# Hybrid decoder block: the last token tile's hidden values row by row, and half of the output sums left in PSUM

## The chip, the cores and the metric

The kernel runs on one core of a Trainium2 chip. The metric is the device time of one execution in microseconds, as the median over runs. The core has five engines with a queue each: TensorE (PE, matmuls; PEld is its weight load), VectorE (DVE), ScalarE (ACT), GpSimd (POOL) and SyncE (SP, which issues DMAs). Each engine works its instructions off in program order, and they wait for each other through semaphores.

## The reference

One decoder block on 1,024 tokens of width 1,024, in float32. The part that matters here is its last one, PEER, a retrieval of experts. Each token is normed to `x`. Eight heads each make a query of 256 numbers, score it against two sets of 128 keys, take the best 16 of each set, and of their 256 sums the best 16. A pair of keys names one of 16,384 experts, so a token has 8 x 16 = 128 picks, with softmax weights `g` in each head:

```python
h = jnp.einsum('td,ted->te', xc, jnp.take(u, ic, axis=0))   # one row of u per pick
a = jax.nn.gelu(h, approximate=False) * gc
return jnp.einsum('te,ted->td', a, jnp.take(v, ic, axis=0)) # one row of v per pick
```

## The kernel before

The 1,024 tokens are eight tiles of 128. Tiles 0 and 1 (`NS = 2`) are done pick by pick: for each of the 128 picks, an indirect DMA fetches a row of `u` for each token (128 rows of 4 KB, 512 KB), and VectorE multiplies by `x` and sums, a "row job"; the same again with rows of `v`. That is 2 x 2 x 128 = 512 row jobs. The other six tiles (768 tokens, `DSEQ`) are done densely: every one of the 128 expert tiles (128 rows of `u` and of `v`) is multiplied with all 768 tokens, in two halves of 384 columns (`DHALF`), and a dense table of weights, mostly zero, selects. A float32 product is three float16 matmuls (`split_mm`, lines 238 to 240). So an expert tile costs 2 x 8 x 3 = 48 matmuls of 384 columns for the hidden values and 36 of 512 columns for the output `y`.

The stages that the change touches run one after another:

- `retrieve` (about 650 to 1055 us of the span). For each head `h` TensorE makes the queries and scores of head `h + 1` while VectorE finds the best 16s of a head. Between them lie 24 expert tiles (`HEAD_TILES`, 2 or 3 for a head and 6 for the last), whose hidden values are computed early, passed through gelu and stored to DRAM. One early tile goes: 8 transposes (`turn`), ScalarE writes the high part and the whole (`split`), GpSimd subtracts for the low part (`low`, line 1423), two halves of 24 matmuls (`hidden`), two gelus. GpSimd's queue for a head is: `low` of the first tile, `low_w` (low part of a query weight, line 1671), `picks` of the head before (line 1678, two products of 2,048 elements), then `low` of each further tile, with `weights` of the head before (line 1683) behind the second. VectorE waits for `weights` of the head before at line 1783.
- `spread_weights` (about 1055 to 1588 us). The dense table is built for four tokens at a step, 192 steps. VectorE makes `same`, `right` and two `left` tiles (lines 1892 to 1898), TensorE multiplies them (line 1918), ScalarE copies them out (line 1965). VectorE may be four steps ahead of TensorE (`RING`). With every four steps goes one early expert tile, 48 in all, handled as above.
- `experts` (from 1588 us). First 56 "late" tiles, whose hidden values are computed here, then the 72 early ones, whose hidden values are read back. Per tile VectorE also multiplies by the table (line 2366), makes low parts (lines 2315 and 2374), adds three finished `y` sums into `h` (`add_y`, line 2323), and does row jobs (lines 2332 and 2342): 2 for each early tile and the rest, 368, over the late ones. GpSimd makes `v_lo` (line 2301) and issues the row fetches (line 2292) into five buffers.

The `y` sums of a group of four tiles have two PSUM banks that take turns; each of the 12 sums of a group is added to `h` before its bank is used again.

## Time and profile before

| | |
|---|---|
| Median of 3 runs | 3084.58 us (3083.65 to 3088.66) |
| Profiled execution | 3081.31 us |
| Its span, first to last instruction | 3079.6 us |
| Mean granted TensorE clock | 0.983 of full |
| TensorE busy | 2968.7 us (96%) |
| VectorE busy | 2313.1 us (75%) |
| GpSimd busy | 1257.6 us (41%) |
| ScalarE busy | 977.5 us (32%) |

The profiled execution has 1.7 us outside its span, and lies 3.3 us under the median. Busy shares are means over stages with different limits, so the prediction reads each stage by itself. A matmul's length in the profile is longer than the distance to the next one, because matmuls overlap.

### The profile page before, as it was taken

The page shows a single profiled execution, that of the slowest core. Times are in us where ns is not written, and L with a number is a line of the kernel's source. Part 1 is how long each engine was busy: PE and PEld are TensorE (multiplying, and loading weights), DVE is VectorE, ACT ScalarE, POOL GpSimd, SP SyncE. Part 2 cuts the span into 40 slices and gives each one's busy share as a digit, 9 for nine tenths or more (in the row PEclk, how much of TensorE's full clock was granted, in tenths as well). Part 3 has the DMA queues.
Part 4 walks back from the last instruction along what each step waited for, and adds up shares of the span by engine and source line. Part 5 has one row for each costly group of instructions (what it writes and reads, how often), then busy time and mean ns, then how long its engine had stood idle before and what let it go on. Part 6 is the DMA issues. An engine that isn't in the chain of part 4 may idle for free. (4 is left out here: it accounts for less than half of the span.)

```text
span 3079.6 us, 46779 instructions
## 1 busy us (share of the span) xinstructions
PE 2968.7 (96%) x17450; PEld 1663.7 (54%) x17450; DVE 2313.1 (75%) x4663; ACT 977.5 (32%) x1417; POOL 1257.6 (41%) x883
## 2 busy tenths in 40 slices
PE   7989998989999799999999999999999999999999
PEld 4445465455555577777765555555555544444444
DVE  3255376358888666666649999989999999999996
ACT  4332365134433344444432222222222222222221
POOL 1013121014243311211226666676666666566562
PEclk9999899999999899999999999999999999999999
DMA  3110100121211245545568989989999888888884
GB/s 101 55 55 15 55 1 28 62 74 63 83 56 61 93 166 198 189 176 199 188 227 290 310 302 329 316 303 315 307 308 322 290 312 296 303 298 299 300 299 168
DMA packets 258490, 601.37 MB, mean 195 GB/s; under 512 B 21025, under 2 KB 127665, under 8 KB 255281
## 3 DMA queue, kind: packets, MB, share of 16 engines
q1 hardware_dynamic: 181168, 321.78, 31.0%
q0 software_dynamic: 73728, 268.47, 24.3%
q10 hardware_dynamic: 3456, 9.44, 0.8%
q8 instruction: 69, 1.13, 0.1%
q14 instruction: 69, 0.56, 0.1%
HBM read 516.78 MB, written 82.84 MB: 195 GB/s over the span
## 5 line engine op out<-in xcount | busy, mean ns | idle before, releaser
L238 PE MATMUL f_y<-f_v_hi,f_a_hi 128*128 128x512 f16 x1536 | 582.4, 379 | 8.7 <-DVE p_h L2323 8.7
L239 PE MATMUL f_y<-f_v_lo,f_a_hi 128*128 128x512 f16 x1536 | 582.1, 379 | 0.0
L240 PE MATMUL f_y<-f_v_hi,f_a_lo 128*128 128x512 f16 x1536 | 582.1, 379 | 0.0
L2292 POOL DMA_INDIRECT x_rows<-in_peer_v,p_row_index x256 | 305.9, 1195 | 281.6 <-DVE p_h L2342 256.2
L2292 POOL DMA_INDIRECT x_rows<-in_peer_u,p_row_index x251 | 321.7, 1282 | 186.4 <-DVE x_rows L2332 141.9
L2332 DVE SCALAR_TENSOR_TENSOR x_rows<-x_rows,p_xs 128x1024 f32<-128x1024 f32 x256 | 378.4, 1507 | 24.7 <-DMA x_rows<-in_peer_u,p_row_index 24.5
L2342 DVE SCALAR_TENSOR_TENSOR p_h<-x_rows,f_row_a,p_h 128x1024 f32<-128x1024 f32 x256 | 384.5, 1502 | 16.6 <-DMA x_rows<-in_peer_v,p_row_index 11.4
L2301 POOL TENSOR_TENSOR f_v_lo<-f_v_in,f_v_hi 128x1024 f16<-128x1024 f32 x128 | 286.8, 2241 | 87.4 <-ACT f_v_hi L2240 85.4
L2323 DVE SCALAR_TENSOR_TENSOR p_h<-f_y,p_h 128x512 f32<-128x512 f32 x384 | 262.4, 683 | 75.9 <-PE f_y L240 75.4
L238 PE MATMUL f_hid<-p_act_hi,x_u_hi 128*128 128x384 f16 x880 | 286.9, 326 | 2.1 <-DVEq L2308 2.1
L240 PE MATMUL f_hid<-p_act_hi,x_u_lo 128*128 128x384 f16 x880 | 286.9, 326 | 0.0
L239 PE MATMUL f_hid<-p_act_lo,x_u_hi 128*128 128x384 f16 x880 | 286.9, 326 | 0.0
L1894 DVE TENSOR_TENSOR e_right<-p_iota,p_picked_all 128x512 f16<-128x512 f32 x192 | 132.1, 688 | 188.0 <-PE e_tab L1918 188.0
L1423 POOL TENSOR_TENSOR e_u_lo<-e_u_all,e_u_hi 128x1024 f16<-128x1024 f32 x48 | 106.5, 2218 | 402.6 <-ACT e_u_all L1417 402.6
L238 PEld LDWEIGHTS f_y<-f_v_hi,f_a_hi 128*128 128x128 f16 x1536 | 150.2, 98 | 196.4 <-DVE p_h L2323 21.3
L238 PE MATMUL e_hid<-p_act_hi,e_u_hi 128*128 128x384 f16 x768 | 251.5, 327 | 4.1 <-POOL e_u_lo L1423 4.1
L239 PE MATMUL e_hid<-p_act_lo,e_u_hi 128*128 128x384 f16 x768 | 251.4, 327 | 0.0
L240 PE MATMUL e_hid<-p_act_hi,e_u_lo 128*128 128x384 f16 x768 | 251.4, 327 | 0.0
L240 PEld LDWEIGHTS f_y<-f_v_hi,f_a_lo 128*128 128x128 f16 x1536 | 150.3, 98 | 181.1
L239 PEld LDWEIGHTS f_y<-f_v_lo,f_a_hi 128*128 128x128 f16 x1536 | 150.3, 98 | 175.3
L2252 ACT ACTIVATE f_a_hi<-x_gel 128x768 f16<-128x768 f32 x128 | 107.6, 841 | 343.9 <-DVE x_gel L2366 343.9
L2240 ACT ACTIVATE f_v_hi<-f_v_in 128x1024 f16<-128x1024 f32 x128 | 134.9, 1054 | 214.8 <-DMA f_v_in<-in_peer_v 199.6
(314 smaller groups left out, 5489.5 us busy)
## 6 DMA issues: line engine op xcount, KB each, us to landing
f_v_in<-in_peer_v SPq DMA_DIRECT2D x128, 512.0 KB, 5.6
dense_weights<-e_stage SPq DMA_DIRECT2D x24, 2048.0 KB, 7.6
f_g_in<-dense_weights SPq DMA_DIRECT2D x32, 1536.0 KB, 16.2
x_u_in<-in_peer_u SPq DMA_DIRECT2D x56, 512.0 KB, 6.2
x_gel<-early_tiles SPq DMA_DIRECT2D x72, 384.0 KB, 3.5
e_u_in<-in_peer_u SPq DMA_DIRECT2D x48, 512.0 KB, 4.1
early_tiles<-e_gel SPq DMA_DIRECT2D x48, 384.0 KB, 2.3
a_w_in<-in_w_in SPq DMA_DIRECT2D x24, 512.0 KB, 3.7
```

Of the source, the lines that this page charges most:

```text
L238: pe.matmul(out, a_hi, b_hi, start=first, stop=False)
L239: pe.matmul(out, a_hi, b_lo, start=False, stop=False)
L240: return pe.matmul(out, a_lo, b_hi, start=False, stop=last)
L1423: self.nc.gpsimd.tensor_tensor(self.u_lo[b][:], self.u_all[:], self.u_hi[b][:], ALU.subtract).then_inc(self.u_lo_done, 1)
L1894: nc.vector.tensor_tensor(right[r][:], lanes(T.iota[:], 1, P, BANK_T, P), lanes(key1_t[:, toks], 2, P, BANK_T, P), ALU.is_equal)
L2240: nc.scalar.activation(v_hi[m // GROUP][m % GROUP][:], v_in[m % 2][:], ACT.Copy).then_inc(v_hi_done, 1)
L2252: nc.scalar.activation(a_hi[m // GROUP][m % GROUP][:], gel[m % 2][:], ACT.Copy).then_inc(a_hi_done, 1)
L2292: nc.gpsimd.indirect_dma_start(out=rows[q % ROWS][:], out_offset=None, in_=table, in_offset=bass.IndirectOffsetOnAxis(ap=T.row_index[:, ti ...
L2301: nc.gpsimd.tensor_tensor(v_lo[g][j][:], v_in[m % 2][:], v_hi[g][j][:], ALU.subtract).then_inc(v_lo_done, 1)
L2323: nc.vector.scalar_tensor_tensor(T.h[:, NS + t, cols], y[k % 2][:], 1.0 / S_A, T.h[:, NS + t, cols], ALU.mult, ALU.add).then_inc(y_added, 1)
L2332: nc.vector.scalar_tensor_tensor(row, row, 1.0, T.xs[:, tile, :], ALU.mult, ALU.mult, accum_out=row_hid[:, tile, pick:pick + 1]).then_inc( ...
L2342: nc.vector.scalar_tensor_tensor(T.h[:, tile, :], row, row_a[:, tile, pick:pick + 1], T.h[:, tile, :], ALU.mult, ALU.add).then_inc(row_use ...
```

## The change

1. The last token tile (tile 7, `HT`) leaves the dense product with `u`. The hidden matmuls of all 128 expert tiles go over 640 tokens (`HID`), in halves of 320 columns (`HHALF`). The output matmuls stay at six tiles.
2. Its 128 hidden values per token come from rows of `u`. The first 58 picks (`HELD_JOBS`) are done in `retrieve`, in heads 2 to 7, in up to five slots of two picks per head: GpSimd issues the fetch into one of two buffers and multiplies by `x` (`fetch`, `product`), ScalarE sums the row (`add_up`). The other 70 are row jobs of VectorE in the first 146 of the 192 steps of `spread_weights`. At the end of block 9 the values are passed through gelu, weighted, transposed and put in the place of tile 7's weights, so that the table holds finished values for these tokens; in `experts` ScalarE copies them (`held`).
3. In `spread_weights` the low part of an early tile is made by VectorE from PSUM, GpSimd only issues fetches, and the two `left` products are one instruction of twice the size.
4. In the early tiles of `experts`, the six `y` sums with odd `k` stay in PSUM banks freed by the hidden values (`resident`), over all groups, and are added to `h` once at the end. VectorE does 5 row jobs for two early tiles in place of 4, so 332 in place of 368 remain for the late tiles.

```diff
 # class EarlyTiles
-        toks = slice(NS * P + half * DHALF, NS * P + (half + 1) * DHALF)
+        toks = slice(NS * P + half * HHALF, NS * P + (half + 1) * HHALF)
...
+    def split_high(self, act, c, b):
+        n = c * self.ring + b
+        act.wait_ge(self.u_turned, n + 1)
+        act.wait_ge(self.hid_done, BASE + 2 * (n - self.ring) + 2)
+        self.nc.scalar.activation(self.u_hi[b][:], self.u_ps[:], ACT.Copy, scale=S_U).then_inc(self.u_hi_done, 1)
+
+    def low_from_bank(self, dve, c, b):
+        n = c * self.ring + b
+        dve.wait_ge(self.u_hi_done, n + 1)
+        self.nc.vector.scalar_tensor_tensor(self.u_lo[b][:], self.u_ps[:], S_U, self.u_hi[b][:], ALU.mult,
+                                            ALU.subtract).then_inc(self.u_lo_done, 1)
 # retrieve
+        def jobs(h, slot):
+
+            pair = (h - 2) * 5 + slot
+            return [q for q in (2 * pair, 2 * pair + 1) if 0 <= q < HELD_JOBS]
 # retrieve, ScalarE
+            def add_up(h, slot):
+                for q in jobs(h, slot):
+                    act.wait_ge(held_product, q + 1)
+                    nc.scalar.activation(rows[q % 2][:], rows[q % 2][:], ACT.Copy,
+                                         accum_out=T.h_hid[:, q:q + 1]).then_inc(held_sum, 1)
...
                 E.split(act, *of_head[0])
+                add_up(h - 1, 4)
                 if h + 2 < PEER_H:
                     split_w(h + 2, h % 2)
                 if h + 1 < PEER_H:
                     act.wait_ge(scored, 4 * h + 4)
                     queries_out(h + 1)
+                    add_up(h, 0)
                     scores_out(h + 1)
+                else:
+                    add_up(h, 0)
+                add_up(h, 1)
                 for i, (c, b) in enumerate(of_head):
...
                     E.keep(act, c, b)
+                    if i < 2:
+                        add_up(h, 2 + i)
 # retrieve, GpSimd
+            def fetch(h, slot):
+                for q in jobs(h, slot):
+                    pool.wait_ge(held_index, q // TOPK + 1)
+                    if q >= 2:
+                        pool.wait_ge(held_sum, q - 1)
+                    nc.gpsimd.indirect_dma_start(
+                        out=rows[q % 2][:], out_offset=None, in_=io.peer_u[0],
...
+            def product(h, slot):
+                for q in jobs(h, slot):
+                    pool.wait_ge(held_loaded[q % 2], 16 * (q // 2 + 1))
+                    nc.gpsimd.tensor_tensor(rows[q % 2][:], rows[q % 2][:], T.xs_h[:],
+                                            ALU.mult).then_inc(held_product, 1)
...
+                fetch(h, 0)
                 E.low(pool, *of_head[0])
+                product(h, 0)
+                fetch(h, 1)
                 if h + 2 < PEER_H:
                     low_w(h + 2, h % 2)
+                product(h, 1)
+                fetch(h, 2)
                 if h:
                     picks(h - 1)
                 for i, (c, b) in enumerate(of_head[1:]):
                     E.low(pool, c, b)
-                    if h and i == 0:
-                        weights(h - 1)
+                    if i == 0:
+                        product(h, 2)
+                        if h:
+                            weights(h - 1)
+                        fetch(h, 3)
+                    if i == min(1, len(of_head) - 2):
+                        product(h, 3)
+                        fetch(h, 4)
+                product(h, 4)
 # spread_weights, VectorE
-                nc.vector.tensor_tensor(left[r][:, 0], same[s % 2][:], each(w_hi), ALU.mult)
-                nc.vector.tensor_tensor(left[r][:, 1], same[s % 2][:], each(w_lo), ALU.mult).then_inc(built, 1)
...
+                nc.vector.tensor_tensor(left[r][:], lanes(same[s % 2][:], 1, P, 2, P, BANK_T),
+                                        lanes(w[:, :, toks], 2, P, 2, P, BANK_T), ALU.mult).then_inc(built, 1)
+
+                if n % 4 == 0 and n // 4 < EARLY_S * NBLOCK:
+                    E.low_from_bank(dve, *ring_at(n // 4 // EARLY_S, n // 4 % EARLY_S))
+                if n < JOB_STEPS:
+                    for q in range(UJOBS * n // JOB_STEPS, UJOBS * (n + 1) // JOB_STEPS):
+                        row_job(q)
 # spread_weights, TensorE
+            def turn_held(blk):
+                pe.wait_ge(h_a_done, 1)
+                pe.wait_ge(E.u_lo_done, BASE + (blk + 1) * EARLY_S)
+                pe.transpose(E.u_ps[:, 0, :], T.h_hid[:], T.ident[:]).then_inc(h_turned, 1)
+                pe.wait_ge(h_out, 1)
 # experts
+        resident = [u_ps[:].rearrange("p k c -> p (k c)")[:, h * HALF:(h + 1) * HALF] for h in range(2)] + [
+            hid_banks[b][:, h, :] for b in range(2) for h in range(2)]
...
-        LATE_JOBS = JOBS - SPREAD_JOBS - 2 * N_EARLY
+        LATE_JOBS = JOBS - SPREAD_JOBS - 5 * N_EARLY // 2
...
+                act.wait_ge(a_lo_done, BASE + n - 1)
+                nc.scalar.activation(gel[m % 2][:, HID:].rearrange("p (b t) -> p b t", t=TB),
...
+                stay = group_n >= RESIDENT
+                if stay and k % 2 and group_n < LAST:
+                    return
```

## Rows read from the trace of the kernel before

**Rows 1.** Windows of four stages: us, busy us (x instructions) of each engine.
```profile
654.00:1055.00 401.00, 382.56 (x2242) 224.83 (x2241) 344.55 (x1848) 148.47 (x191) 141.54 (x54) 1.00 0.19 66
1063.00:1574.00 511.00, 505.68 (x4218) 355.30 (x4217) 314.88 (x763) 239.45 (x383) 112.19 (x53) 0.99 0.50 185
1620.00:2470.00 850.00, 847.53 (x4738) 468.90 (x4736) 777.86 (x930) 187.76 (x209) 566.68 (x414) 1.00 0.91 309
2470.00:3060.00 590.00, 583.78 (x2692) 261.80 (x2691) 547.60 (x520) 135.79 (x145) 339.21 (x218) 1.00 0.83 290
```

**Rows 2.** The page's groups by cost, the two TensorE products.
```profile
L238 PE MATMUL f_y<-f_v_hi,f_a_hi 128*128 128x512 f16 x1536 | 582.4, 379 | 8.7 <-DVE p_h L2323 8.7
...
L238 PE MATMUL f_hid<-p_act_hi,x_u_hi 128*128 128x384 f16 x880 | 286.9, 326 | 2.1 <-DVEq L2308 2.1
```

**Rows 3.** Waits of the retrieval stage, 654 to 1055 us.
```profile
DVE r_weight L1783 <- POOL r_picked L1683: 35.7, 6, 7.8
```

**Rows 4.** Timeline of ScalarE, 843 to 896 us: start, length, operation.
```profile
865.41 0.60 ACT L1617 ACTIVATE r_q_t<-r_bank 128x512 f32<-128x512 f32 x1 [4.58 <-PE r_bank L240]
...
873.75 1.02 ACT L1415 ACTIVATE r_u_hi<-r_u_ps 128x1024 f16<-128x1024 f32 x1 [0.32 <-PE r_u_ps L1407]
```

**Rows 5.** Timeline of GpSimd, 840 to 945 us and at 1040 us.
```profile
846.86 2.14 POOL L1423 TENSOR_TENSOR r_u_lo<-r_u_all,r_u_hi 128x1024 f16<-128x1024 f32 x1 [11.11 <-ACT r_u_all L1417]
850.54 4.07 POOL L1671 TENSOR_TENSOR r_w_lo<-x_gr,r_w_hi 128x2048 f16<-128x2048 f32 x1 [1.54 <-ACT r_w_hi L1611]
854.57 7.62 POOL L1678 TENSOR_TENSOR r_match<-r_match,r_top_f 128x2048 f16<-128x2048 f16 x2
875.84 2.12 POOL L1423 TENSOR_TENSOR r_u_lo<-r_u_all,r_u_hi 128x1024 f16<-128x1024 f32 x1 [13.65 <-ACT r_u_all L1417]
...
885.08 2.13 POOL L1423 TENSOR_TENSOR r_u_lo<-r_u_all,r_u_hi 128x1024 f16<-128x1024 f32 x1 [6.76 <-ACT r_u_all L1417]
898.32 2.14 POOL L1423 TENSOR_TENSOR r_u_lo<-r_u_all,r_u_hi 128x1024 f16<-128x1024 f32 x1 [11.11 <-ACT r_u_all L1417]
...
941.95 2.67 POOL L1423 TENSOR_TENSOR r_u_lo<-r_u_all,r_u_hi 128x1024 f16<-128x1024 f32 x1 [12.17 <-ACT r_u_all L1417]
...
1040.40 2.12 POOL L1423 TENSOR_TENSOR r_u_lo<-r_u_all,r_u_hi 128x1024 f16<-128x1024 f32 x1 [7.12 <-ACT r_u_all L1417]
```

**Rows 6.** Timeline of GpSimd at the end of the spread.
```profile
1563.14 0.94 POOL L1994 DMA_INDIRECT x_rows<-in_peer_u,p_row_index  x1 [0.30 <-issue]
```

**Rows 7.** DMA issues: queue, count, us from issue to landing.
```profile
x_rows<-in_peer_u,p_row_index POOLq DMA_INDIRECT x256, 6.0
```

**Rows 8.** A window of 2 us at the start of the spread.
```profile
1074.00:1076.00 2.00, 2.00 (x8) 0.91 (x6) 0.00 (x0) 0.00 (x0) 0.45 (x1) 0.50 0.00 0
```

**Rows 9.** Timeline of VectorE in the spread, 1300 to 1323 us.
```profile
1302.85 0.69 DVE L1894 TENSOR_TENSOR e_right<-p_iota,p_picked_all 128x512 f16<-128x512 f32 x1 [1.49 <-PE e_tab L1918]
1303.46 0.42 DVE L1897 TENSOR_TENSOR e_left<-e_same,e_w_hi 128x512 f16<-128x512 f16 x1
1303.80 0.42 DVE L1898 TENSOR_TENSOR e_left<-e_same,e_w_lo 128x512 f16<-128x512 f16 x1
...
1304.47 0.68 DVE L1894 TENSOR_TENSOR e_right<-p_iota,p_picked_all 128x512 f16<-128x512 f32 x1
...
1313.32 0.69 DVE L1894 TENSOR_TENSOR e_right<-p_iota,p_picked_all 128x512 f16<-128x512 f32 x1 [1.49 <-PE e_tab L1918]
```

**Rows 10.** The chain of work that ended last, late tiles.
```profile
1650.73 0.87 PE f_u_ps L2173 x8
...
1667.17 0.87 PE f_u_ps L2173 x8
```

**Rows 11.** Timeline of VectorE in the late tiles, 1697 to 1712 us.
```profile
1702.02 1.23 DVE L2315 SCALAR_TENSOR_TENSOR x_u_lo<-f_u_ps,x_u_hi 128x1024 f16<-128x1024 f32 x1
1703.16 3.21 DVE L2332 SCALAR_TENSOR_TENSOR x_rows<-x_rows,p_xs 128x1024 f32<-128x1024 f32 x1
1706.31 0.08 DVE L2332 DVE_READ_ACCUMULATOR x_rows<-x_rows,p_xs 128x1 f32 x1
```

More of the change, by code:

```diff
@@ L1492, in retrieve @@
         picked = [S.sb(f"picked{n}", [P, NT, PICKS]) for n in range(3)]
+        rows = [S.sb(f"rows{b}", [P, D]) for b in range(2)]
         bank = [S.ps(f"bank{r}", [P, 4, NKEYS]) for r in range(4)]
@@ L1516, in retrieve @@
         all_out = S.sem("all_out")
+        held_index = S.sem("held_index")
+        held_loaded = [S.sem(f"held_loaded{b}") for b in range(2)]
+        held_product = S.sem("held_product")
+        held_sum = S.sem("held_sum")
         block = ctx.enter_context(nc.Block())
@@ L1909, in _, with step @@
             pe.sem_inc(spread, BASE)
-            def step(blk, last):
+            def turn_held(blk):
[3 more added lines that the diff above has]
+                pe.wait_ge(h_out, 1)
+            def step(blk, last, held=False):
                 for s in range(STEPS):
@@ L1929, in _ @@
             E.turn(pe, 0, 0)
-            with pe.Fori(0, NBLOCK - 1) as blk:
+            with pe.Fori(0, HBLOCK) as blk:
                 step(blk, False)
-            step(NBLOCK - 1, True)
+            step(HBLOCK, False, held=True)
+            for blk in range(HBLOCK + 1, NBLOCK):
+                step(blk, blk == NBLOCK - 1)
             def turn(b):
@@ L1966, in step @@
                                          tab[r][:].rearrange("p t i -> p i t"), ACT.Copy).then_inc(out, 1)
+                    if held and s == 3:
+                        gelu_held()
                     if s in HALVES:
@@ L2068, in experts @@
         u_ps = S.ps("u_ps", [P, KT, P])
-        hid = [S.ps(f"hid{b}", [P, 2, HALF])[:, :, 0:DHALF] for b in range(2)]
+        hid_banks = [S.ps(f"hid{b}", [P, 2, HALF]) for b in range(2)]
+        hid = [banks[:, :, 0:HHALF] for banks in hid_banks]
         y = [S.ps(f"y{b}", [P, HALF]) for b in range(2)]
@@ L2186, in hidden, with outputs @@
                 last.then_inc(hid_done, 1)
-            def outputs(group_n, g, part):
+            def outputs(group_n, g, part, stay=False, start=True, stop=False):
                 if part == 0:
@@ L2208, in step @@
                 if y_too:
-                    outputs(2 * c + m // GROUP - 1, (m // GROUP + 1) % 2, m % GROUP)
+                    outputs(2 * c + m // GROUP - 1, (m // GROUP + 1) % 2, m % GROUP, stay=early, start=first or not early)
             hidden(1, 1, between=2)
@@ L2218, in _ @@
                 step(LATE - 1, m, u_too=m < LOOP - 1)
-            with pe.Fori(LATE, TURNS) as c:
+            for m in range(LOOP):
+                step(LATE, m, early=True, first=m < GROUP)
+            with pe.Fori(LATE + 1, TURNS) as c:
                 for m in range(LOOP):
@@ L2222, in _ @@
             for part in range(GROUP):
-                outputs(NE // GROUP - 1, 1, part)
+                outputs(LAST, 1, part, stay=True, start=False, stop=True)
         @block.scalar
```

194 lines of the change are left out of this document (139 added, 55 removed).

## The prediction

> **What bounds the kernel now.** I read the page first, then cut the run into its stages by windows, because the busy shares of the page average over them. The windows [rows 1] give four stretches. In the retrieval TensorE is busy 382.6 of 401 us, in the spread 505.7 of 511, in the late tiles 847.5 of 850, in the early tiles 583.8 of 590. So TensorE bounds all four. The second engine differs: VectorE has 344.6 of 401 us in the retrieval, 314.9 of 511 in the spread, 777.9 of 850 and 547.6 of 590 behind it; GpSimd is nowhere a bound, but the reader should see that 141.5 us of 401 in the retrieval is little only as long as nobody waits for its order. The waits of that stage already show VectorE standing 35.7 us for GpSimd's `weights` [rows 3]. DMA takes 0.91 and 0.83 of its engines in the two expert stretches, at 309 and 290 GB/s [rows 1].
>
> **What a narrower hidden product gives.** A matmul of 512 columns lasts 379 ns and one of 384 columns 326 ns [rows 2]: 53 ns for 128 columns, 26.5 ns for the 64 that fall away. 48 matmuls make 1.27 us per expert tile, 163 us for 128 tiles, if TensorE stays the bound. That is the gross gain; the rest of the sum is what each stage gives back.
>
> **Retrieval: 24 tiles, minus 30 us of TensorE, plus 58 picks.** GpSimd gets 58 fetches, 1.24 us each (0.94 long and 0.30 to the next [rows 6]), and 58 products. No row has a float32 product of two SBUF tiles there; the nearest, `low` with the same 1,024 elements, is 2.13 us [rows 5], so I take that (bounds: 2.1, and 4.07, the length of `low_w` [rows 5]). ScalarE gets 58 sums; a copy of 1,024 elements lasts 1.02 us there [rows 4], and reading the sum out comes on top, I take 1.25 (VectorE's row job, product and all, is 1.22 [rows 11]). The busy time fits (58 x 3.4 = 196 us on GpSimd); the order does not. Each pair of fetches waits for the sums of the pair before, and these stand at fixed places in ScalarE's queue. I follow the head whose first `low` starts at 846.86 [rows 5], with all else at its old time. ScalarE has the last query bank out at 866.0 (the one at 865.41, 0.60 long [rows 4]) and only then sums slot 0: 867.2. GpSimd fetches slot 1 until 869.7, does `low_w` (4.07) until 873.8, the first row has landed after 6.0 us [rows 7] at 873.2, the products end at 878.1, and the second sum at 879.4. ScalarE stands in front of the first gelu until then. GpSimd waits with the second fetch of slot 2, until 880.6, then does `picks` (7.6 us [rows 5]), which before ran directly behind `low_w`. So `low` of the second tile starts at 888.2, not 875.84: TensorE is out of work from about 876 on and waits 12 us. The third tile: products of slot 2 to 894.6, sums to 895.9, gelu (0.5) and split (two copies of 1.0 [rows 4]) to 898.4, not 885.08. Two narrower halves of 3.3 us, turn and split later the next head's first `low` could start at 910.1, not 898.32: plus 12 us. A head with two tiles (898.32 to 941.95, 43.6 us) misses the last stretch: TensorE ends at 897, so the head takes 53, plus 9.5, but slots 3 and 4 are then still open, which hands 2.5 us to the next head. Heads 2 to 6 have 2, 3, 3, 2 and 3 tiles: 9.5 + 14.5 + 12 + 9.5 + 12.5 = 58. The last head has no queries that hide slots 0 and 1. Each is a round of fetch, landing, products and sum of about 10 us, and slot 2 comes on top: about 22 us until the `low` that stood at 1040.40. Heads 0 and 1 have no picks and gain 5 x 1.27 = 6. Sum: plus 74 us. What is late next: VectorE gets `weights` later by the same 16 us, but it then has a period of 63 us for its 43 us of work (344.6 in eight heads), so it isn't the bound.
>
> TensorE now stands idle twice in a head. After the idle stretch between the two stages the granted clock is 0.50, which is 1.2 GHz, and eight matmuls take 2 us even while it is fully busy [rows 8]. Most of the second tile's first half would be slow, but ScalarE is still at the sums then. I put 4 us for all heads. The Trainium skill (TensorE: Matmul & The Clock Gate, HAM oscillation) says that an array that waits in every round of a loop starts cold every round; by it I would put some 2 us on the path for each of eleven stalls, 22 us and not 4. The rows show such a cold spell at the stage's start, and no repeated one.
>
> **Spread: 48 tiles.** A tile with its four steps takes TensorE 1313.32 - 1302.85 = 10.47 us [rows 9]; less 1.27 is 9.2. VectorE needs 1.62 us for a step (1302.85 to 1304.47 [rows 9]), of which the two `left` are 0.34 each. One instruction of double size saves only a start: 0.60 for 0.68, step 1.54, four steps 6.2. The low part from PSUM is 1.14 (1702.02 to 1703.16 [rows 11]), and 70 x 4 / 146 = 1.92 row jobs of 1.15 (1.22 long, overlapping its successor by 0.07 [rows 11]) are 2.2. Sum 9.5: VectorE takes over as the bound by a little, for 36.5 tiles. 36.5 x 9.5 + 11.5 x 9.2 = 453 us against 48 x 10.47 = 503: minus 50. At the start GpSimd's slow first `low` goes, minus 4; at block 9 transpose and copy of the held values stop TensorE for some 2. Minus 52. If the merged product lost its rate, the nearest row is `right` with 0.61 for 512 elements, 1.2 for 1,024 [rows 9]. The skill (VectorE: DVE Perf Modes, What auto-detection actually checks) gives two elements a cycle to 16-bit tensors of step 1, which the merged one still is.
>
> **Late tiles.** The period is 1667.17 - 1650.73 = 16.44 us [rows 10], TensorE alone; it becomes 15.17. VectorE: 332/52 = 6.4 row jobs in place of 7.1, and one of them stretched by GpSimd's product (3.21 for 1.22 [rows 11]): 7.3 + 2.0 for rows, 1.8 for three `add_y`, 1.1, 0.75 and 0.9 for the others, 13.9 of 15.17, as tight as now. DMA: 512 KB each of `u` and `v`, 384 of the table and 6.4 x 512 of rows, 4.79 MB in 15.17 us, 316 GB/s where 309 stand now. 55 x 1.27 = 70, less 6 for slips: minus 64. ScalarE's `held` copy is hidden; its engine is busy 188 of 850 us [rows 1].
>
> **Early tiles.** 2,692 matmuls are 75 portions of 36 in 590 us, 7.9 us each, 99% TensorE. The resident sums take nothing from TensorE. They free 1.5 x 0.6 us of VectorE, which the half row job more (0.6) nearly takes back. Traffic rises to 2.56 MB in 7.9 us, 324 GB/s for 290. I take 0, bounds minus 5 and plus 68 (below).
>
> **Sum.** 74 + 4 - 52 - 64 = minus 38. 3081.3 - 38 = 3043; the median lies 3.3 above the profiled execution: 3047.
>
> **Rivals.** (a) The slots are covered: sums come out as soon as products end, and `picks` finds GpSimd free. For it speaks that GpSimd is idle 260 of 401 us. Against it the fixed place of the sums behind the query banks. The retrieval then keeps its gain of 30 us, at most plus 10: 2943 to 2983. (b) GpSimd's work is stretched by VectorE, which shares its ports: fetches of 2.0 us and products of 3.1. On the path of a head lie four fetches and six products, 10 us more in each of six: 3107, slower. It decides the sign from 6 us per head on. The stretched pair at 1703.16 [rows 11] speaks for it, but the best-16 searches that fill VectorE there have no second SBUF tensor. The skill's rule (GPSIMD Engine Reference, Engine selection) would put such products on VectorE, twice as fast; 58 x 1.15 = 67 us there, where 56 are idle. (c) DMA becomes the bound of `experts`: 4.79 MB at 309 GB/s is 15.5 us, plus 18 over the late tiles, and 2.56 MB at 290 is 8.8, plus 68 over the early: 3133; half of it 3090. (d) The merged product runs at half its rate: step 2.1 for 1.54, a tile 11.7, plus 82: 3129. (e) Gains and losses cancel within what a measurement can tell (0.2%, 6 us): 3078 to 3091.
>
> **Chances.** Forecast 0.52 (3020 to 3077); (a) 0.13; (b) 0.10; (c) 0.12, a third of it still faster; (d) 0.05; (e) 0.08. Faster 0.52 + 0.13 + 0.04 + a little of (b) = 0.71, same 0.08, slower 0.21. The range 2990 to 3105 leaves out most of (a), (d) and the full (c).
>
> **What would show it.** In the retrieval: GpSimd's second `low` of a head 12 us later after its first, ScalarE waiting for GpSimd products, TensorE busy under 80%, granted clock below 1.00. In the spread: a tile period near 9.5 with VectorE over 90% busy and TensorE waiting for it. Late period 15.2. Early period unchanged at 7.9 with DMA share over 0.9. Wrong it would be if the period of a middle head stayed at 51 us, or the early portions grew past 8.2.

## The result

| | Median | Range | Against before |
|---|---|---|---|
| Kernel before, same chip | 3086.27 us | 3083.65 to 3088.87 | |
| Kernel after | 3100.18 us | 3093.86 to 3106.81 | 1.0045 [1.0027, 1.0062] |

The change makes the kernel slower by 0.45%. The forecast was 3047 us and faster; the sign is wrong, the time lies near the upper end of the range. The profiled execution after took 3093.86 us, with a span of 3092.2.

The places in the trace where one stage hands over to the next tell where the time went. The starts are those of the spread's first table matmul, of the first hidden matmul of `experts` and of the last late one.

| Stage | before | after | difference | predicted |
|---|---|---|---|---|
| up to the spread's first table matmul | 1062.9 | 1158.3 | +95.4 | +78 |
| spread, to the first late hidden matmul | 527.1 | 470.9 | -56.2 | -52 |
| late tiles, first to last hidden matmul | 876.9 | 820.2 | -56.7 | -64 |
| the rest of the span, early tiles | 612.7 | 642.8 | +30.1 | 0 |
| sum (span) | 3079.6 | 3092.2 | +12.6 | -38 |

Each column comes from one profiled execution, and executions of one kernel differ. The first `low` of the retrieval starts at 655.9 us before and at 649.2 after, though the change does not touch what runs ahead of it; over the fourteen profiles of this document it starts between 648.4 and 657.7 us. So 6.7 us of the first row are scatter in the new kernel's favour: from first `low` to first table matmul the stage went from 407.0 to 509.1 us, plus 102.1.

### The profile page after: what moved, and what is told of

Same layout as the page of the kernel before. It is cut to its first block and busy times, and to the rows that moved or that the text cites. A ratio compares the mean times of both kernels' runs of the same rounds, so it can differ in the third digit from the quotient of the medians.

```text
span 3092.2 us, 46939 instructions
## 1 busy us (share of the span) xinstructions
PE 2828.5 (91%) x17451; PEld 1673.5 (54%) x17451; DVE 2371.1 (77%) x4563; ACT 1012.8 (33%) x1615; POOL 1418.8 (46%) x1021
## 3 DMA queue, kind: packets, MB, share of 16 engines
q8 instruction: 77, 1.26, 0.2%
## 5 line engine op out<-in xcount | busy, mean ns | idle before, releaser
L246 PE MATMUL f_y<-f_v_hi,f_a_hi 128*128 128x512 f16 x1080 | 410.7, 380 | 40.8 <-DVE f_a_lo L2561 33.5
L247 PE MATMUL f_y<-f_v_lo,f_a_hi 128*128 128x512 f16 x1080 | 410.7, 380 | 0.0
L248 PE MATMUL f_y<-f_v_hi,f_a_lo 128*128 128x512 f16 x1080 | 410.7, 380 | 0.0
L246 PE MATMUL f_hid<-p_act_hi,x_u_hi 128*128 128x320 f16 x880 | 264.6, 301 | 2.0 <-DVEq L2489 2.0
L247 PE MATMUL f_hid<-p_act_lo,x_u_hi 128*128 128x320 f16 x880 | 264.6, 301 | 0.0
L248 PE MATMUL f_hid<-p_act_hi,x_u_lo 128*128 128x320 f16 x880 | 264.5, 301 | 0.0
L246 PE MATMUL r_hid<-p_act_hi,r_u_hi 128*128 128x320 f16 x384 | 123.5, 322 | 128.0 <-POOL r_u_lo L1433 128.0
L246 PE MATMUL e_hid<-p_act_hi,e_u_hi 128*128 128x320 f16 x768 | 230.2, 300 | 0.0
L247 PE MATMUL e_hid<-p_act_lo,e_u_hi 128*128 128x320 f16 x768 | 230.2, 300 | 0.0
L248 PE MATMUL e_hid<-p_act_hi,e_u_lo 128*128 128x320 f16 x768 | 230.1, 300 | 0.0
L1745 POOL TENSOR_TENSOR r_rows<-r_rows,p_xs_h 128x1024 f32<-128x1024 f32 x58 | 136.3, 2360 | 23.7 <-DMA r_rows<-in_peer_u,p_h_index 23.4
```

Of the source, the lines that this page charges most:

```text
L246: pe.matmul(out, a_hi, b_hi, start=first, stop=False)
L247: pe.matmul(out, a_hi, b_lo, start=False, stop=False)
L248: return pe.matmul(out, a_lo, b_hi, start=False, stop=last)
L1745: nc.gpsimd.tensor_tensor(rows[q % 2][:], rows[q % 2][:], T.xs_h[:], ALU.mult).then_inc(held_product, 1)
```

## The profile after

First the windows of the stages, with the columns of [rows 1].

```profile
core 0: us, PE busy (x) PEld busy (x) DVE busy (x) ACT busy (x) POOL busy (x), PEclk, DMA share, GB/s
640.00:1140.00 500.00, 371.36 (x2251) 232.85 (x2250) 346.19 (x1853) 206.00 (x306) 331.53 (x168) 0.87 0.34 110
1160.00:1510.00 350.00, 342.14 (x3198) 271.52 (x3199) 350.00 (x615) 147.84 (x254) 65.56 (x70) 0.99 0.85 305
1510.00:1616.00 106.00, 105.22 (x1010) 84.18 (x1008) 84.42 (x150) 45.21 (x82) 0.00 (x0) 1.00 0.53 195
1630.00:2450.00 820.00, 807.50 (x4907) 487.43 (x4906) 731.70 (x902) 203.47 (x276) 521.03 (x382) 0.99 0.89 307
2450.00:3070.00 620.00, 586.48 (x2691) 262.93 (x2690) 537.02 (x448) 152.91 (x219) 402.50 (x254) 0.99 0.84 299
```

In the retrieval TensorE stands idle for 129 of 500 us, where it had 18 of 401 idle, and its mean clock is 0.87 in place of 1.00. No other engine is full either: GpSimd has 332 of 500. That is the picture of a wait, not of a bound. In the spread VectorE is busy 350 of 350 us: it is the bound, as forecast. In the early tiles TensorE falls from 99% to 94.6%, and the DMA share hardly moves, 0.84 for 0.83 [rows 1]. These windows hold the end of the stage too, where the loads run out. Without it, before and then after:

```profile
2480.00:3020.00 540.00, 534.54 (x2465) 239.60 (x2464) 510.15 (x482) 128.79 (x138) 323.60 (x207) 1.00 0.86 301
2480.00:3020.00 540.00, 510.69 (x2341) 228.84 (x2340) 469.94 (x391) 135.21 (x193) 360.13 (x227) 0.99 0.86 306
```

The share is the same 0.86, and 5 GB/s more go with TensorE at 94.6% for 99.0%.

The waits of the retrieval (waiting instruction, whom it waits for: us in all, times, the longest):

```profile
ACT r_rows L1670 <- POOL r_rows L1745: 155.6, 44, 11.3
PE r_hid L246 <- POOL r_u_lo L1433: 128.0, 17, 19.6
DVE r_weight L1862 <- POOL r_picked L1729: 119.6, 7, 26.6
POOL r_rows L1737 <- ACT r_rows L1670: 43.6, 22, 13.9
```

The 129 idle us of TensorE are one row, 128.0 us for GpSimd's `low`. ScalarE waits 155.6 us for products, in front of its own gelu and split. One head with two tiles (head 5), with the same columns as [rows 5]; its first `low` is at 941.43, the next head's at 1003.23:

```profile
941.43 2.14 POOL L1433 TENSOR_TENSOR r_u_lo<-r_u_all,r_u_hi 128x1024 f16<-128x1024 f32 x1
943.53 4.66 POOL L1745 TENSOR_TENSOR r_rows<-r_rows,p_xs_h 128x1024 f32<-128x1024 f32 x2
952.87 0.98 POOL L1737 DMA_INDIRECT r_rows<-in_peer_u,p_h_index  x1 [4.69 <-ACT r_rows L1670]
954.16 0.94 POOL L1737 DMA_INDIRECT r_rows<-in_peer_u,p_h_index  x1 [0.30 <-issue]
955.12 4.08 POOL L1717 TENSOR_TENSOR r_w_lo<-x_gr,r_w_hi 128x2048 f16<-128x2048 f32 x1
959.15 4.65 POOL L1745 TENSOR_TENSOR r_rows<-r_rows,p_xs_h 128x1024 f32<-128x1024 f32 x2
...
966.70 7.62 POOL L1724 TENSOR_TENSOR r_match<-r_match,r_top_f 128x2048 f16<-128x2048 f16 x2
974.26 2.13 POOL L1433 TENSOR_TENSOR r_u_lo<-r_u_all,r_u_hi 128x1024 f16<-128x1024 f32 x1
976.34 4.65 POOL L1745 TENSOR_TENSOR r_rows<-r_rows,p_xs_h 128x1024 f32<-128x1024 f32 x2
...
986.01 4.71 POOL L1745 TENSOR_TENSOR r_rows<-r_rows,p_xs_h 128x1024 f32<-128x1024 f32 x2 [2.13 <-DMA r_rows<-in_peer_u,p_h_index]
990.87 0.98 POOL L1737 DMA_INDIRECT r_rows<-in_peer_u,p_h_index  x1 [0.15 <-DVE p_h_index L1825]
992.67 1.87 POOL L1737 DMA_INDIRECT r_rows<-in_peer_u,p_h_index  x1 [0.82 <-ACT r_rows L1670]
995.43 2.35 POOL L1745 TENSOR_TENSOR r_rows<-r_rows,p_xs_h 128x1024 f32<-128x1024 f32 x1 [0.89 <-DMA r_rows<-in_peer_u,p_h_index]
997.96 2.35 POOL L1745 TENSOR_TENSOR r_rows<-r_rows,p_xs_h 128x1024 f32<-128x1024 f32 x1 [0.18 <-DMA r_rows<-in_peer_u,p_h_index]
...
1003.23 2.13 POOL L1433 TENSOR_TENSOR r_u_lo<-r_u_all,r_u_hi 128x1024 f16<-128x1024 f32 x1
```

The same two `low` of this head before:

```profile
927.29 2.13 POOL L1423 TENSOR_TENSOR r_u_lo<-r_u_all,r_u_hi 128x1024 f16<-128x1024 f32 x1 [13.64 <-ACT r_u_all L1417]
941.95 2.67 POOL L1423 TENSOR_TENSOR r_u_lo<-r_u_all,r_u_hi 128x1024 f16<-128x1024 f32 x1 [12.17 <-ACT r_u_all L1417]
```

The reader is to see two things. GpSimd waits 4.69 us with the second pair of fetches until ScalarE has summed the first pair, which stands behind the query banks, and `picks` then stands in front of `low`. Even so the second `low` comes only 3.8 us later after the first than before, 32.8 us for 29.0. The larger part of this head's loss lies behind it: 29.0 us to the next head's first `low` in place of 14.7, because the products of slots 2, 3 and 4 and their fetches all stand ahead of that `low`. Before, GpSimd waited 12 us for its data there; now it is busy 50.1 of the head's 61.8 us. ScalarE's split for the second `low` had been done at 967.1. While TensorE waits for that `low` the clock falls. Windows of 4 us, the clock is the third value from the end:

```profile
966.00:970.00 4.00, 0.00 (x0) 0.00 (x0) 0.00 (x0) 1.46 (x3) 3.99 (x2) 0.50 0.80 201
974.00:978.00 4.00, 1.55 (x6) 0.89 (x7) 0.00 (x0) 0.00 (x0) 4.00 (x3) 0.50 0.00 0
982.00:986.00 4.00, 4.00 (x33) 3.15 (x32) 3.97 (x5) 0.94 (x4) 1.53 (x2) 1.00 0.61 177
```

The page's chain of work that ended last, which here reaches back to the start of `experts`, shows the early tiles. After:

```profile
PE 18%; DVE 11%; DMA 10%; issue 6%; SPq 1%; ACT 1%; POOL 1%; DVEq 0%; ACTq 0%
```

Six of the ten per cent of DMA are the loads of `v`. Before, the same line of the page had PE 36% and DMA 4%.

## The experiments

Twelve kernels ran, in three groups. In each, the kernel before ran on the same chip (medians 3087.85, 3085.20 and 3086.78 us). "Spread at" is the first table matmul, "spread", "late" and "early" are the three other lengths of the table above, in us of the profiled execution. That execution is not always near the median: it lies 14.7 us above it in `order38` and 9 us below it in `order38_s` and `fit28`. The late and early columns differ by some 10 us between kernels that are alike there (818 to 830 and 642 to 651), so differences of that size say nothing by themselves.

| Run | Median | Ratio | Spread at | spread | late | early |
|---|---|---|---|---|---|---|
| before | 3086.27 | 1 | 1062.9 | 527.1 | 876.9 | 612.7 |
| after | 3100.18 | 1.0045 [1.0027, 1.0062] | 1158.3 | 470.9 | 820.2 | 642.8 |
| resident_only | 3126.19 | 1.0125 [1.0106, 1.0143] | 1066.3 | 526.9 | 875.9 | 658.0 |
| tile7_only | 3110.25 | 1.0079 [1.0060, 1.0099] | 1162.1 | 472.6 | 865.3 | 612.3 |
| half_v | 3076.66 | 0.9953 [0.9933, 0.9974] | 1165.7 | 472.5 | 830.2 | 609.6 |
| held28 | 3077.14 | 0.9970 [0.9955, 0.9986] | 1105.1 | 508.2 | 818.5 | 642.0 |
| order58 | 3086.03 | 1.0002 [0.9986, 1.0018] | 1146.7 | 472.4 | 819.3 | 647.2 |
| order38 | 3066.73 | 0.9938 [0.9917, 0.9960] | 1103.2 | 496.0 | 829.6 | 650.9 |
| held8 | 3074.26 | 0.9963 [0.9945, 0.9981] | 1073.0 | 531.9 | 826.3 | 647.6 |
| after_2jobs | 3103.68 | 1.0078 [1.0049, 1.0106] | 1154.0 | 472.4 | 862.6 | 605.7 |
| order38_s | 3048.25 | 0.9880 [0.9856, 0.9905] | 1083.3 | 494.3 | 818.0 | 642.0 |
| fit28 | 3046.96 | 0.9874 [0.9852, 0.9897] | 1065.5 | 508.1 | 819.0 | 643.3 |
| fit28_s | 3052.28 | 0.9888 [0.9867, 0.9910] | 1071.3 | 508.0 | 822.2 | 645.9 |
| left_split | 3115.95 | 1.0098 [1.0060, 1.0135] | 1160.8 | 482.3 | 821.2 | 645.8 |

### The two halves of the change apart

`resident_only` is the kernel before with the resident sums and their five row jobs for two early tiles; `tile7_only` is the kernel after without them.

```diff
 # tile7_only, against after
-        LATE_JOBS = JOBS - SPREAD_JOBS - 5 * N_EARLY // 2
+        LATE_JOBS = JOBS - SPREAD_JOBS - 2 * N_EARLY
...
 # and outputs, add_y and the final wait of SP as in before
```

> The kernel before with one part of the change alone: the six odd y sums stay in PSUM through the early tiles, and VectorE does 5 row jobs for two early tiles (332 for the late ones). The hidden products stay at 768 tokens, and the retrieval and the spread stay as they were. Traffic theory (the expert tiles are held by DMA at about 300 GB/s, the rate at which the early tiles ran in the kernel before, 2.36 MB in 7.9 us, and in the changed one, 2.56 MB in 8.5 us): an early tile moves 2.62 MB, so it takes 8.7 us and not 7.9, plus 60 us over 72 tiles; the late tiles stay at TensorE's 16.44 us; total about 3145. Order theory (the early tiles are held by GpSimd, VectorE and the load queue waiting for each other, and the resident sums relieve it; what slowed them in the changed kernel is the picks' side): the early tiles stay at 7.9 us, total 3080 to 3090.

> The changed kernel without the resident sums: all 12 y sums go through two banks as before, and VectorE does 4 row jobs for two early tiles, 368 for the late ones. Traffic theory: an early tile moves 2.29 MB, TensorE holds it again at 7.9 us, minus 42 us against the changed kernel; a late tile moves 5.15 MB, which at 310 GB/s takes 16.6 us where TensorE needs 15.17, so the late tiles take what they took before the change, plus 50 to 65 us; total 3105 to 3120. Order theory (late tiles are held by TensorE alone, which lost 1.27 us a tile): the late tiles stay at about 15.2 us and the early ones go back to 7.9, total about 3060.

Alone, the resident sums cost 45 us in the early tiles and give nothing in the late ones, though these have 36 row jobs less. Without them the early tiles run as before, 612.3 us, but the late tiles fall back to 865.3: of the 70 us that the narrower products give there, 12 are left. So each half does little without the other: the row jobs that leave the late tiles let the narrower products take effect, and cost time among the early ones. In all, the resident half is worth 10 us to the kernel with tile 7 (3110 against 3100). Both runs fit the traffic theory; of the two totals it wanted, 3105 to 3120 came (3110), and for about 3145 it was 3126, since the early tiles lost 45 us and not 60.

### Is it the traffic?

In `half_v` the loads of `v` from the second turn on bring only the first 512 of 1,024 columns, so half of `y` is built from stale rows; everything else is as in after. In `after_2jobs` only the number of row jobs goes back to four for two early tiles.

```diff
 # half_v
-                    sp.dma_start(v_in[m % 2][:], v_v[view, m]).then_inc(v_loaded[m % 2], 16)
+                    cols = slice(0, D if first else HALF)
+                    sp.dma_start(v_in[m % 2][:, cols], v_v[view, m][:, cols]).then_inc(v_loaded[m % 2], 16)
```

> The changed kernel, but in experts the load of a tile's v rows brings only the first 512 of the 1,024 columns from the second group of eight tiles on (the other half of the buffer keeps old values; this part of y is left wrong). No instruction less on any engine, 0.26 MB less in each tile. Traffic theory: early tiles 2.29 MB, back to 7.9 us; late tiles to 15.2; experts from 1463 to about 1415 us, total about 3050. Order theory: no change beyond the shorter landing of v, total 3090 to 3100.

> The kernel after with four row jobs to two early tiles, as before, in place of five; the sums stay resident. The late tiles get the 37 jobs. Traffic theory (at the bytes per tile of the kernel before the early tiles run as they did): early to end 610 to 618 us in place of 643, but the late tiles then carry the bytes of the run with tile 7 alone and go from 820 to about 865: 3100 to 3118, no gain, because the bytes of the whole stage decide. Order theory (the resident sums themselves, their places in TensorE's and VectorE's order, cost the early tiles their 30 us): early to end stays near 640, and with the slower late tiles the kernel takes 3135 to 3145.

The windows of the early tiles, first `half_v`:

```profile
2468.00:3060.00 592.00, 586.99 (x2718) 265.17 (x2716) 545.66 (x450) 152.29 (x219) 409.10 (x254) 1.00 0.83 282
```

then `after_2jobs`, late and early:

```profile
1628.00:2490.00 862.00, 819.58 (x4901) 489.20 (x4899) 781.99 (x937) 203.78 (x277) 552.55 (x416) 0.98 0.91 313
2490.00:3060.00 570.00, 568.59 (x2632) 256.62 (x2630) 493.50 (x408) 152.51 (x219) 335.86 (x220) 1.00 0.83 290
```

With half of each `v` load gone and nothing else changed, the early tiles take 609.6 us for 642.8, and TensorE is back at 99%. The resident sums and all row fetches are still there, and VectorE's busy time is the same (546 us of 592, 537 of 620). So the 30 us are the price of transfers, not of the order of the sums. The waits show the path. The first two rows are of the early tiles after (2450 to 3070 us), the last two of `half_v` (2468 to 3060):

```profile
PE f_y L246 <- DVE f_a_lo L2561: 33.5, 15, 3.5
DVE x_gel L2553 <- DMA x_gel<-early_tiles: 43.3, 17, 4.1
PE f_y L246 <- DVE f_a_lo L2562: 4.9, 6, 1.3
DVE x_gel L2554 <- DMA x_gel<-early_tiles: 18.1, 15, 2.1
```

TensorE waits for VectorE's low parts, and VectorE for the hidden values that are read back. In the chain of work that ended last, within the early tiles, the loads of `v` make up 28.9% after, 14.3% in `half_v` and 12.4% before. In `after_2jobs` the early tiles take 605.7 us with the resident sums in place, 7 less than before, so the order theory, which wanted 640, falls. For the traffic it says less than `half_v`, because with 36 row jobs go their 512 KB each as well as their time on VectorE: there VectorE waits even longer for the read values, 47.1 us, but is busy 494 of 570 us, catches up, and TensorE loses 1.3 us to it. `half_v` as a whole took 3077 us; about 3050 was wanted, since the late tiles gave nothing. What is taken out of the early tiles is paid in the late ones: plus 42.4 us for 36 row jobs, 1.18 us each. There the cause is left open: that is VectorE's own time for a row job (1.21 us) as well as 512 KB at 444 GB/s, `half_v` did not make the late tiles of the kernel after faster (830.2 for 820.2, within the scatter), and no run here gives the crowded late tiles of `tile7_only` less traffic alone.

### Fewer picks in the retrieval

```diff
-HELD_JOBS = 58
+HELD_JOBS = 28      # held8: 8
```

> The changed kernel with 28 picks of tile 7 in the retrieval (heads 2, 3 and four slots of head 4) and 100 in the spread in place of 58 and 70. Slot theory (each head with slots loses its 12 to 20 us because sums and products stand ahead of the gelu and of picks in their queues): heads 5, 6 and 7 return to the period of TensorE, 41 to 47 us and some 50 for the last, so the retrieval ends some 55 us earlier, while the spread takes 30 row jobs more at 1.15 us, plus 35; total 20 us less, about 3080. Rival (the loss is one of TensorE's clock and of GpSimd's load as a whole, spread over all heads): the retrieval gives back only its share of the picks' GpSimd time, 30 x 3.6 / 2, and the spread takes 35: no gain, 3095 to 3105.

> The kernel after with 8 picks in the retrieval in place of 58, in the old order, and 50 more row jobs in the spread. By held28 a pick in heads 5 to 7 cost 53 / 30 = 1.8 us of the retrieval and 37.5 / 30 = 1.25 us in the spread. If the slots of heads 3 and 4 cost as much, the spread starts at 1105 - 36 = 1069 and lasts 508 + 25 = 533: 3066. If the first 28 picks cost what they add up to against the kernel before (42 us plus the 30 us of narrower products, 72 / 28 = 2.6 us each), it starts at 1053: 3050. If fetches from memory bound the spread (rather than VectorE), its share passes 0.95 and it takes over 545 us: above 3080.

`held28` moves 30 picks of heads 5 to 7 to the spread: the retrieval gets 53.2 us shorter and the spread 37.3 longer, 1.77 us for a pick in the one and 1.24 in the other. Counted from each run's own first `low`, the retrieval is 57.2 us shorter, 1.91 for a pick. A pick in GpSimd's free time costs more of the kernel than one on the engine that bounds the next stage. The slot theory wanted about 3080, and 3077 came. `held8` does not go on like this: its spread starts at 1073.0 us and lasts 531.9, as its first branch had it (1069 and 533), and the kernel gains only 3 us more (3066 was wanted), within the two intervals. Its eight picks all stand in head 2, which has two tiles and still takes 63.8 us from first `low` to first `low` where it had 43.6: 2.5 us for a pick, more than the 1.8 of heads 5 to 7. With its fifth slot, in the kernel after, the head takes 71.4.

### The places in the queues

```diff
 # order58, ScalarE: slot 0 inside queries_out(h + 1), ahead of its third bank; slot 1 behind the split
-                    add_up(h, 0)
                     scores_out(h + 1)
-                add_up(h, 1)
...
                         E.split(act, *of_head[i + 1])
+                    if i == 0:
+                        add_up(h, 1)
 # order58, GpSimd
                 product(h, 0)
-                fetch(h, 1)
                 low_w(h + 2, h % 2)
-                product(h, 1)
-                fetch(h, 2)
+                fetch(h, 1)
                 picks(h - 1)
+                product(h, 1)
                 E.low(pool, c, b)
+                    fetch(h, 2)
+                    weights(h - 1)
                     product(h, 2)
```

> The kernel after with its 58 picks, only the places in two queues changed: ScalarE sums slot 0 between the second and the third query bank and slot 1 behind the split of the second tile, GpSimd does low_w and picks between the two first products and fetches slot 2 behind the second low. Queue-place theory (the retrieval's loss comes from sums that hold up the first gelu and the split, and from products ahead of picks and low): a middle head then goes at GpSimd's own busy time, about 57 us (10 products of 2.35, 10 fetches of 1.25, three low of 2.13, low_w 4.1, picks 7.6, weights 3), in place of 61.8 to 66.6, and the start of the spread moves from 1158 to about 1125 to 1135; the kernel takes 3070 to 3080. Work theory (it is the amount of GpSimd's and ScalarE's work, or its stretching by VectorE, whatever the order): within 6 us of 3100. Spread, late and early tiles as they were, 471, 820 and 643 us.

> order58 with 38 picks in four slots of a head instead of 58 in five; the other 20 are row jobs of the spread. Queue-place theory: GpSimd's work in a middle head is 50 us, TensorE is not held up for long, heads 2 to 5 take about 50 us each and the last head, now without picks, 55: the spread starts at about 1056 to 1070, and takes 471 + 20 x 1.25 = 496 us; the kernel takes 3023 to 3040. Work theory: on the line between held28 (3077) and the kernel after (3100), about 3085.

`order58` has the same work as after and is 14 us faster, so places matter and the work theory (within 6 us) falls. But the spread starts only 11.6 us earlier (15.0 from the first `low` on), not 23 to 33, the kernel misses its 3070 to 3080, and `order38` misses its own upper bound by 27 us as well. A middle head of `order38` shows what had come in place of the old wait. GpSimd, then VectorE, then ScalarE, each from its own timeline:

```profile
985.99 7.63 POOL L1726 TENSOR_TENSOR r_match<-r_match,r_top_f 128x2048 f16<-128x2048 f16 x2
993.58 4.64 POOL L1747 TENSOR_TENSOR r_rows<-r_rows,p_xs_h 128x1024 f32<-128x1024 f32 x2
```

```profile
986.11 12.27 DVE L1848 CAST r_top_f<-r_top_i 128x256 f16<-128x256 uint32 x1
```

```profile
998.42 2.06 ACT L1662 ACTIVATE p_picked_all<-r_bank 128x512 f32<-128x512 f32 x4 [13.18 <-DVE r_top_f L1848]
```

VectorE's small copy of the found places lasts 12.27 us, exactly as long as the four GpSimd products that run without a gap beside it (7.63 + 4.64); in the first head, with GpSimd idle, it lasts 0.29. The kernel after has one such copy too, of 7.0 us, in head 3. ScalarE waits for it with the scores, and behind the scores stand gelu and split. My new order had put the four products next to each other. Two experiments test that:

```diff
 # order38_s: the scores are freed ahead of the copy
-                nc.vector.tensor_copy(top_f[:, h % 2], top_i[:]).then_inc(s_used, 1)
+                dve.sem_inc(s_used, 1)
+                c.step(nc.vector.tensor_copy(top_f[:, h % 2], top_i[:]))
 # fit28, GpSimd of a head; slots: 2, 3, 3, 2, 3, 1 in heads 2 to 7
+                fetch(h, 0)
                 E.low(pool, *of_head[0])
+                picks(h - 1)
+                product(h, 0)
+                fetch(h, 1)
+                low_w(h + 2, h % 2)
+                product(h, 1)
                 E.low(pool, c, b)            # second tile
+                    fetch(h, 2)
+                    weights(h - 1)
                 E.low(pool, c, b)            # third tile
+                    product(h, 2)
```

> order38 with one thing changed: VectorE frees the scores (s_used) before its copy of the found places to top_f, not behind it. In order38 this copy of 256 columns took 0.29 us alone but 12.3 to 12.8 us in four heads, as long as picks and product of GpSimd that ran on without a gap beside it (7.63 + 4.64 = 12.27), and ScalarE waited 38.5 us for it with the queries' banks, the first gelu and the split behind it. Wait theory (what is lost in the reordered head is ScalarE's wait): the spread starts at 1065 to 1080 in place of 1103, the kernel takes 3030 to 3045. VectorE theory (with the blocked copies VectorE itself has 57 to 58.5 us of each 60 and is the bound, wherever ScalarE waits): the spread starts at 1095 or later, the kernel is within 8 us of order38's 3067.

> 28 picks as in held28, but laid out to fit TensorE's head: two slots in a head with two tiles, three in a head with three, one in the last; picks directly behind the first low, a fetch between the run of GpSimd's products and low_w, sums between the query banks, behind the second split and behind the second tile. Place theory: GpSimd reaches the second low 29 us after the first, TensorE never waits long, heads 2 to 6 take 224 to 245 us in all (289 in order38, 325 in the kernel after, 240 before) and the spread starts at 1035 to 1055 in place of held28's 1105; spread 508, the rest as held28: the kernel takes 3010 to 3030. If a pick costs its 1.8 us wherever it stands, the spread starts at 1105 and the kernel takes 3077.

> fit28 with the early s_used of order38_s as well. If the blocked copy still holds up ScalarE in fit28, this is up to 20 us faster than fit28; if the new places keep GpSimd's run short beside it, the two are within 4 us.

`order38_s` changes only what waits for the copy, and gives 18 us of the kernel and, from first `low` to first table matmul, 14.8 of the retrieval (449.7 to 434.9). That is the wait theory, though a little short of it: the spread start (1083.3) and the kernel (3048) lie 3 us past the 1065 to 1080 and the 3030 to 3045 it wanted, and clear of VectorE's 1095 and 3059. `fit28` has held28's 28 picks, and its spread starts 39.6 us earlier, 1065.5, so picks cost by their places; the kernel is faster than before by 1.26%. Two things changed against `held28`, the order in the queues and how many slots each head has, and no run takes them apart. It did not reach the 1035 to 1055 and the 3010 to 3030 that were wanted, and heads 2 to 6 take 252.6 us, not 224 to 245. GpSimd in head 4 of `fit28`:

```profile
842.93 2.14 POOL L1434 TENSOR_TENSOR r_u_lo<-r_u_all,r_u_hi 128x1024 f16<-128x1024 f32 x1 [4.43 <-ACT r_u_all L1428]
845.03 7.62 POOL L1726 TENSOR_TENSOR r_match<-r_match,r_top_f 128x2048 f16<-128x2048 f16 x2
852.61 4.67 POOL L1747 TENSOR_TENSOR r_rows<-r_rows,p_xs_h 128x1024 f32<-128x1024 f32 x2
857.43 0.98 POOL L1739 DMA_INDIRECT r_rows<-in_peer_u,p_h_index  x1
...
864.24 4.66 POOL L1747 TENSOR_TENSOR r_rows<-r_rows,p_xs_h 128x1024 f32<-128x1024 f32 x2
868.86 2.18 POOL L1434 TENSOR_TENSOR r_u_lo<-r_u_all,r_u_hi 128x1024 f16<-128x1024 f32 x1
```

and its middle heads as a window:

```profile
740.00:1000.00 260.00, 229.34 (x1383) 142.41 (x1382) 246.64 (x1202) 116.00 (x169) 178.14 (x87) 0.95 0.35 114
```

In this head the second `low` comes 25.9 us after the first, sooner than the 29.0 of before. It is the best of the five: in heads 2 to 6 it is 28.4, 34.0, 25.9, 35.0 and 28.5 us, and heads 3 and 5 take 59.8 and 51.0 us where they had 50.9 and 43.6. Beside that VectorE is nearly full, 246.6 of 260 us busy with TensorE at 229.3. `fit28_s` gives nothing more (3052 and 3047, intervals that overlap), and its waits say why: ScalarE then waits as long for VectorE to come to the release, 25.6 us in three waits, as it had waited for the copy, 24.2 us in three.

### The merged product of the spread

```diff
 # left_split
-                nc.vector.tensor_tensor(left[r][:], lanes(same[s % 2][:], 1, P, 2, P, BANK_T),
-                                        lanes(w[:, :, toks], 2, P, 2, P, BANK_T), ALU.mult).then_inc(built, 1)
+                nc.vector.tensor_tensor(left[r][:, 0], same[s % 2][:], each(w_hi), ALU.mult)
+                nc.vector.tensor_tensor(left[r][:, 1], same[s % 2][:], each(w_lo), ALU.mult).then_inc(built, 1)
```

> The kernel after with the two products left of the spread apart again, as before. VectorE theory (VectorE bounds the spread at its busy 350 of 350 us): each of the 146 steps that it bounds takes 0.08 us more by the starts (2 x 0.34 against 0.60), at most 0.155 by the busy times (2 x 0.417 against 0.679): 12 to 23 us, the kernel takes 3112 to 3123. If transfers (DMA share 0.85) or TensorE (342 of 350) bound the spread, within 5 us of 3100.

The kernel is 15.8 us slower than after, and its spread 11.4 us longer, inside the 12 to 23 by the first number and just under it by the second. VectorE bounds the spread; TensorE at 342 of 350 us and a DMA share of 0.85 do not.

## Why the prediction was wrong, step by step

- **What bounds each stage, and the gain of 26.5 ns for 64 columns: right.** A hidden matmul of the late tiles takes 299 ns (median) where it took 326, 27 for 26.5.
- **Spread, minus 52: right** in mechanism and size (minus 56.2). The 146 steps that VectorE bounds took 350 us, 9.6 us for a tile where 9.5 was forecast, and the other 46 took 106, the 9.2 of the forecast; the 4 us that it gave beyond the forecast lie at the ends of the stage. The merged product is 0.679 us long where each of the two was 0.417. VectorE's waits for TensorE fell from 188.0 to 14.9 us. Rival (d), half the rate, is out.
- **Late tiles, minus 64: nearly right** (minus 56.7). Over 55 tiles that is 1.03 us each of the 1.27. TensorE is busy 807.5 of 820 us, 12.5 idle, where it had 2.5 idle of 850 [rows 1]. `tile7_only` shows that the gain hung on the 36 row jobs that leave the stage; the sum had them out of it, but did not say that they decide it.
- **Retrieval, plus 74 and plus 4 for the clock: the second step that failed, "slots 3 and 4 are then still open, which hands 2.5 us to the next head"** (plus 95.4, or 102.1 without the 6.7 us of scatter ahead of the stage). Heads 2 to 6 cost 84.6 us, not 58. The two with two tiles cost 27.8 and 18.2, not 9.5 each: slots 3 and 4 run there one behind the other, some 10 us each for fetch, landing, product and sum, and all of it stands ahead of the next head's first `low`, 14.3 us in both heads. The three heads with three tiles cost 12.5, 15.1 and 11.0 us (38.6 in all; forecast 14.5, 12 and 12.5). That these agree is in part luck: their second `low` was to come 12 us later after the first, and it came 3.8, 5.3 and -0.8 us later; 6.8, 8.2 and 9.6 us of the loss lie between the last `low` and the next head's first. So the rule was right, that sums and products at fixed places hold up `low`, and the place at which it costs most was wrong. The last head, up to the first table matmul, costs 23.2, about the 22 of the forecast, and heads 0 and 1 give 5.5, about the 6. Rival (a), covered slots, is out; rival (b), stretched GpSimd work, too: a product takes 2.35 us for the 2.13 taken, a fetch 0.94 to 0.98.
- **The clock.** The prediction had TensorE idle twice in a head, in eleven stalls. It stands idle for long once in a head: 15.0 to 19.6 us in front of the second tile of heads 2 to 7, and 15.3 in front of the last head's first, seven times in all, and behind each the granted clock was 0.50. The mean is 0.87 over the retrieval. TensorE is busy 371.4 us there; before it was 382.6 [rows 1], less 30 by the narrower products would be 353. So 19 us of its busy time are the slower clock; how much of them lies on the path no run separates. The Trainium skill (TensorE: Matmul & The Clock Gate, HAM oscillation) has an array that waits in every round of a loop start cold in every round, and the trace agrees, 0.50 in every head from 2 on. The 22 us of the prediction lie nearer to the 19 than its 4 do, but they were eleven stalls of an assumed 2 us each, and here are seven.
- **Early tiles, "I take 0": the first step that failed.** The sum wanted 324 GB/s and I let that pass, set against a mean of 290 that holds the end of the stage, where loads run out; away from the end 301 GB/s went before. What came was 306 GB/s at a DMA share of 0.86. The 2,691 matmuls of the window are 74.8 portions in 620 us, 8.29 us each for 7.89, past the 8.2 that the prediction had named as its sign of being wrong, and 72 tiles by 0.40 are 29 us. `half_v`, with the bytes taken out again, gives them back. It is rival (c), in the early tiles only, at a little under half of the 68 us of its bound. Its chance of 0.12 was too low: the prediction's own rows already had the late tiles at 309 GB/s and no stretch above it.

The sum of the misses: 17.4 (retrieval) + 30.1 (early) + 7.3 (late) - 4.2 (spread) = 50.6 us, which is the way from minus 38 to plus 12.6. Without the 30 us of the early tiles the span would have been 17.5 us shorter than before, without the 17.4 of the retrieval 4.8 shorter, which is less than a measurement can tell: the early tiles are the larger miss and decide the sign, and the retrieval takes the larger part of what is then left. In the retrieval 6.7 us of luck hide a miss of 24.

That the kernel can be had faster than before is shown by `fit28`, 3047 us. It keeps everything of the change and lays 28 picks, not 58, where TensorE's head leaves room; its early tiles still take 643.3 us.

## What to carry to other kernels

When work is put into an engine's idle time, its queue places count, not its sum: write down for the shortest round of the loop what stands ahead of the instruction that the bounding engine waits for, the first one of the next round included, and let the number of pieces in each round follow from that. When a change moves bytes from one stage to another, take the highest rate that the trace shows in a stage of the same mix as the limit; if the sum wants more, that is a loss to be priced, and a DMA share of 0.84 to 0.86 is no proof of room. A second look at the reordered kernel's longest instruction, not only at its waits, finds an operation that is held up by another engine.

## What the runs showed of the hardware

- A VectorE copy of 256 columns (uint32 to float16) takes 0.29 us alone and 11.7 to 12.8 us in four heads of `order38` beside unbroken GpSimd products. In the kernel before it is 2.9 to 3.3 us in four of eight heads, three times beside `picks` and once beside `low_w`. Each long copy ends 0.1 to 0.2 us behind the end of a GpSimd instruction. In the four heads of `order38` that is the last of four instructions on two program lines; but in head 1 of the same run the copy ends (2.32 us) behind the first of two products, with the second running on. What decides between the two is open. VectorE's searches for the best eight, in the same heads, keep their 262 to 276 ns over 128 elements. The Trainium skill (SBUF — State Buffer, SBUF: two separate sides) has an exclusive lock on ports that GpSimd shares with some operations of VectorE, held for the whole instruction. The ends of the copies agree with it; that a copy waits over four instructions is more than it says.
- Of 512 KB loads mixed with row fetches, 307 GB/s came in the late tiles of the kernel after at a DMA share of 0.89, where the sum wanted 316, and 306 away from the end of the early tiles at 0.86 (299 and 0.84 with it), where it wanted 324. The highest of the windows shown is 313, at 0.91. The kernel before moved 301 GB/s at the same 0.86 with TensorE at 99.0%. So the rate at which transfers begin to cost time does not show as a full share.
